# Retention states of the sample tokens: outer products on TensorE, or spread rows and DVE

## The reference

```
S_new[d, e] = gamma * S[d, e] + k[d] * v[e]
o[e]        = sum over d of q[d] * S_new[d, e]
```

## Time and profile before

| what | value |
|---|---|
| median of three runs | 935.5 us |
| the profiled execution | 933.9 us |
| its span in the trace | 932.3 us |
| PE busy in the span | 806.9 us (87%) |
| DVE busy | 429.8 us (46%) |
| ACT busy | 219.1 us (23%) |
| POOL busy | 73.9 us (8%) |

### The profile page before, as it was taken

One profiled execution on the slowest core, in us unless ns is written; L12 is line 12 of the kernel. 1 busy time (PEld: TensorE's weight loads), 2 busy tenths in 40 slices (PEclk: granted clock), 3 DMA queues, 4 the chain that ended last, 5 costly groups with the idle time before them and its releaser, 6 DMA issues. The chain is left out here.

```text
span 932.3 us, 13436 instructions
## 1 busy us (share of the span) xinstructions
PE 806.9 (87%) x5047; PEld 573.3 (61%) x5047; DVE 429.8 (46%) x994; ACT 219.1 (23%) x445; POOL 73.9 (8%) x71
## 2 busy tenths in 40 slices
PE   3689999999999999999999998937677788777984
PEld 2467887877977878878878876511653344324421
DVE  3153556547547546546555565782421232123224
ACT  3132505405314324324235041001100000000002
POOL 0000000000000000000000008950000000000000
PEclk9899999999999999999999999978589898889887
DMA  9834224224124224233242140110899999999961
GB/s 285 250 98 138 84 69 117 67 67 139 49 65 138 72 85 116 69 94 90 67 119 87 67 171 9 70 72 23 338 414 416 417 420 416 416 415 419 418 271 47
DMA packets 112603, 167.49 MB, mean 180 GB/s; under 512 B 7633, under 2 KB 91691, under 8 KB 103996
## 3 DMA queue, kind: packets, MB, share of 16 engines
q1 hardware_dynamic: 108876, 158.96, 47.3%
q0 software_dynamic: 1664, 4.98, 1.8%
q10 hardware_dynamic: 2032, 3.13, 1.0%
HBM read 158.63 MB, written 8.43 MB: 179 GB/s over the span
## 5 line engine op out<-in xcount | busy, mean ns | idle before, releaser
L275 PE MATMUL bank<-room,wall 128*128 128x264 f32 (+1 forms) x1152 | 287.2, 395 | 11.2 <-PEq L140 7.2
L275 PEld LDWEIGHTS bank<-room,wall 128*128 128x128 f32 x1152 | 212.3, 192 | 57.0 <-issue 15.3
L1553 PE MATMUL bank<-ring,xg 128*32 128x512 f32 x512 | 72.7, 732 | 35.5 <-DMA ring<-in_expert_w_up_dram 34.5
L1553 PEld LDWEIGHTS bank<-ring,xg 128*32 128x32 f32 x512 | 20.4, 132 | 87.0 <-issue 87.0
L1529 PEld LDWEIGHTS bank<-G,xn 128*128 128x128 f32 x384 | 44.9, 197 | 9.6 <-issue 5.9
L1529 PE MATMUL bank<-G,xn 128*128 128x128 f32 x384 | 46.4, 283 | 3.6 <-DVE GW L1777 3.6
L1805 DVE SCALAR_TENSOR_TENSOR th<-th,bank 128x256 f32<-128x256 f32 x8 | 3.4, 421 | 97.1 <-ACT th L1651 97.1
L1590 PE MATMUL bank<-y,GT 128*128 128x512 f32 x96 | 45.8, 612 | 1.0 <-issue 0.9
L275 PE MATMUL bank<-wall,merged 128*128 128x512 f32 (+1 forms) x96 | 44.4, 613 | 2.5 <-DVE merged L1314 2.5
L1794 DVE TENSOR_TENSOR x<-x,bank 128x512 f32<-128x512 f32 (+1 forms) x48 | 32.8, 684 | 12.2 <-PE bank L1590 12.2
L1112 POOL DMA_DIRECT2D out_rwkv_p_dram<-zout x8 | 4.9, 616 | 397.3 <-ACT zout L836 396.6
(11 more groups left out here) (366 smaller groups left out, 1316.4 us busy)
## 6 DMA issues: line engine op xcount, KB each, us to landing
wall<-in_w_in_dram SPq DMA_DIRECT2D x72, 512.0 KB, 3.6
ring<-in_expert_w_gate_dram SPq DMA_DIRECT2D x32, 1024.0 KB, 17.6
ring<-in_expert_w_up_dram SPq DMA_DIRECT2D x32, 1024.0 KB, 18.6
ring<-in_expert_w_down_dram SPq DMA_DIRECT2D x32, 1024.0 KB, 22.8
room<-in_state_ret_dram SPq DMA_DIRECT2D x8, 512.0 KB, 4.8
out_ret_s_dram<-room POOLq DMA_DIRECT2D x8, 512.0 KB, 3.8
wall<-in_w_out_dram SPq DMA_DIRECT2D x8, 512.0 KB, 3.5
room<-in_state_rwkv_dram SPq DMA_DIRECT2D x1, 2048.0 KB, 8.6
```

Of the source, the lines that this page charges most:

```text
L275: return nc.tensor.matmul(out, lhsT, rhs, start=start, stop=stop, skip_group_check=loose)
L1553: last = mm(MB[e * CAP:(e + 1) * CAP, :], xg[:, b, kk, e * CAP:(e + 1) * CAP], w, start=(kk == 0), stop=(kk == KT - 1))
```

## The change

The value rows alone are transposed (the key column is used where it stands, one channel per partition). ACT copies them to v8 and POOL writes v8 to a scratch row in memory, waits until it has landed, and loads it back spread over all 128 partitions as vrows (128 x 1024). ACT scales sin_ by gamma in place. DVE then forms snew with eight instructions of 128 columns, each with one column of kr as its scalar. On TensorE the outer products are gone and both halves of GB stand ahead of the snew wait; on ACT the tanh of GB stands ahead of the os_ copy; on DVE the snew step stands behind the sample copies (L1066) and the back part's merge (L1070 to L1077). In out_pass the two new DMAs stand between the zout store and the stp store. The constant diag8 and its load (L335) are gone.

The diff, without the lines on that constant:

```diff
@@ -452,8 +447,9 @@
         kvt = buf("kvt", [P, 4, P])
         vd = buf("vd", [P, TT, P])
         sc = buf("sc", [P, TP + P])
-        ks8 = buf("ks8", [B, 2, P])
-        vdiag = buf("vdiag", [B, B, P])
+        v8 = buf("v8", [B, P])
+        vrows = buf("vrows", [P, B, P])
+        scr_v = nc.dram_tensor("scr_v", [KT, B * P], F32, kind="Internal").ap()
         stp = buf("stp", [P, P])
         os_, osq, ors = ys, ysq, yrs
         oc = tok("oc")
@@ -729,8 +725,7 @@
                 for m, src in enumerate((kr[:, 0:P], kr[:, P:TP], vr[:, 0:P], vr[:, P:TP])):
                     last = nc.tensor.transpose(v4(M[3])[:, m, :], src, ident[:])
                 last.then_inc(sem("kvt_mm"), 1)
-                nc.tensor.transpose(M[0][0:B, 0:P], kr[:, TP:T], ident[:])
-                nc.tensor.transpose(M[0][0:B, P:2 * P], vr[:, TP:T], ident[:]).then_inc(sem("kv8_mm"), 1)
+                nc.tensor.transpose(M[0][0:B, 0:P], vr[:, TP:T], ident[:]).then_inc(sem("v8_mm"), 1)
                 project(pe, i, U_GA, 1)
             if back:
                 past(pe, "y_sq", n)
@@ -743,16 +738,12 @@
                 done(pe, "vd_ready", i)
                 mm(pe, M[4][:, 0:P], kvt[:, 0, :], vd[:, 0, :], True, False)
                 mm(pe, M[4][:, 0:P], kvt[:, 1, :], vd[:, 1, :], False, True).then_inc(sem("stp_mm"), 1)
-                done(pe, "vdiag_ready", i)
-                vflat = vdiag[:].rearrange("b c d -> b (c d)")
-                mm(pe, M[0][:, :], ks8[:, 0, :], vflat[:, 0:512], True, True)
-                mm(pe, M[3][:, :], ks8[:, 0, :], vflat[:, 512:1024], True, True).then_inc(sem("kv_mm"), 1)
                 project(pe, i, U_GB, 0)
+                project(pe, i, U_GB, 1)
                 done(pe, "snew_ready", i)
                 for b in range(B):
                     last = mm(pe, M[5][:, TP + b:TP + b + 1], snew[:, b, :], qr[:, TP + b:TP + b + 1], False, True, True)
                 last.then_inc(sem("o_mm"), 1)
-                project(pe, i, U_GB, 1)
                 done(pe, "o_copy", i)
                 mm(pe, M[0][:, 0:T], mean128[:], os_[:], True, True).then_inc(sem("omean_mm"), 1)
 
@@ -835,10 +826,13 @@
                 act.wait_ge(sem("zout_free"), n)
                 A.copy(zout[:], M[0][0:HD, 0:P].rearrange("p (h c) -> p h c", h=2)).then_inc(sem("zt_copy"), 1)
             if front:
+                done(act, "v8_mm", i)
+                last_pass(act, "v8_sent", 16 * i)
+                A.copy(v8[:], M[0][0:B, 0:P]).then_inc(sem("v8_ready"), 1)
                 done(act, "kvt_mm", i)
                 A.copy(kvt[:], v4(M[3])).then_inc(sem("kvt_copy"), 1)
-                done(act, "kv8_mm", i)
-                A.copy(ks8[:], M[0][0:B, 0:2 * P].rearrange("p (n c) -> p n c", n=2)).then_inc(sem("ks8_ready"), 1)
+                act.wait_ge(sem("sin_in"), 16 * (i + 1))
+                A.activation(sin_, sin_, ACT.Copy, scale=dcol[:, 2:3]).then_inc(sem("sin_decayed"), 1)
             if back:
                 past(act, "yc_ready", n)
                 A.activation(ysq[:, 0:TP], yc[:, 0:TP], ACT.Square).then_inc(sem("y_sq"), 1)
@@ -852,10 +846,10 @@
                 done(act, "stp_mm", i)
                 last_pass(act, "stp_sent", i * 16)
                 A.copy(stp[:], M[4][:, 0:P]).then_inc(sem("stp_ready"), 1)
+                projected(act, i, U_GB)
+                A.activation(gb[:], pj[1][:, 0:T], ACT.Tanh, scale=0.5).then_inc(sem("gb_tanh"), 1)
                 done(act, "o_mm", i)
                 A.copy(os_[:], M[5][:, 0:T]).then_inc(sem("o_copy"), 1)
-                projected(act, i, U_GB)
-                A.activation(gb[:], pj[1][:, 0:T], ACT.Tanh, scale=0.5).then_inc(sem("gb_tanh"), 1)
                 done(act, "oc_ready", i)
                 A.activation(osq[:], oc[:], ACT.Square).then_inc(sem("o_sq"), 1)
 
@@ -1045,8 +1039,6 @@
                 done(dve, "kvt_copy", i)
                 V.tensor_scalar(vd[:, 0, :], kvt[:, 2, :], dcol[:, 0:1], None, mult)
                 V.tensor_scalar(vd[:, 1, :], kvt[:, 3, :], dcol[:, 1:2], None, mult).then_inc(sem("vd_ready"), 1)
-                done(dve, "ks8_ready", i)
-                V.tensor_tensor(vdiag[:], ks8[:, 1:2, :].broadcast_to([B, B, P]), diag8[:], mult).then_inc(sem("vdiag_ready"), 1)
                 done(dve, "gs_tanh", i)
 
                 V.scalar_tensor_tensor(out=sg[:], in0=thg[:], scalar=1.0, in1=pj[U_GS % 2][:, 0:T], op0=add, op1=mult).then_inc(sem("gs_silu"), 1)
@@ -1054,14 +1046,6 @@
                 past(dve, "y_root", n)
                 V.reciprocal(yrs[:, 0:TP], yrs[:, 0:TP]).then_inc(sem("y_inv"), 1)
             if front:
-                dve.wait_ge(sem("sin_in"), 16 * (i + 1))
-                last_pass(dve, "snew_sent", 16 * i)
-                done(dve, "kv_mm", i)
-                for half, bank in enumerate((M[0], M[3])):
-                    bs = slice(4 * half, 4 * half + 4)
-                    last = V.scalar_tensor_tensor(out=snew[:, bs, :], in0=sin_[:, bs, :], scalar=dcol[:, 2:3], in1=v4(bank), op0=mult, op1=add)
-                last.then_inc(sem("snew_ready"), 1)
-
                 for m, src in enumerate((r, ep, kmod, vx, kk, ba)):
                     V.tensor_copy(svec[:, bass.ds(i, 1), m, :].rearrange("p o b -> p (o b)"), src[:, TP:T]).then_inc(sem("svec_part"), 1)
             if back:
@@ -1077,6 +1061,13 @@
                 V.tensor_tensor(tile, tile, yc[:, 0:TP], add).then_inc(sem("prompt_merged"), 1)
             if front:
 
+                done(dve, "sin_decayed", i)
+                last_pass(dve, "snew_sent", 16 * i)
+                done(dve, "k_rope", i)
+                dve.wait_ge(sem("vrows_in"), 16 * (i + 1))
+                for b in range(B):
+                    last = V.scalar_tensor_tensor(out=snew[:, b, :], in0=vrows[:, b, :], scalar=kr[:, TP + b:TP + b + 1], in1=sin_[:, b, :], op0=mult, op1=add)
+                last.then_inc(sem("snew_ready"), 1)
                 if back:
                     past(dve, f"state{NCH - 1}", n)
                 V.tensor_copy(epc[:], ep[:, C - 1:TP:C])
@@ -1113,6 +1104,14 @@
                 eng.wait_ge(sem("zout_sent"), 16 * n)
                 eng.sem_inc(sem("zout_free"), 1)
             if i is not None:
+                settle(eng)
+                done(eng, "v8_ready", i)
+                eng.dma_start(scr_v[bass.ds(i, 1), :].rearrange("o (b v) -> (o b) v", b=B), v8[:]).then_inc(sem("v8_sent"), 16)
+                last_pass(eng, "snew_ready", i)
+                eng.wait_ge(sem("v8_sent"), 16 * (i + 1))
+                eng.sem_inc(sem("v8_there"), 1)
+                settle(eng)
+                eng.dma_start(vrows[:].rearrange("p b v -> p (b v)"), scr_v[bass.ds(i, 1), :].broadcast_to([P, B * P])).then_inc(sem("vrows_in"), 16)
                 settle(eng)
                 done(eng, "stp_ready", i)
                 eng.dma_start(o["ret_p"][0, 0][bass.ds(i, 1)].rearrange("o k v -> (o k) v"), stp[:]).then_inc(sem("stp_sent"), 16)
```

More of the change, by code:

```diff
@@ L112, in constants @@
     out["slot"] = np.tile(np.arange(CAP)[None, :], (P, 1)).astype(np.float64)
[L113 to L116, removed]
     return {k: np.ascontiguousarray(v.astype(np.float32)) for k, v in out.items()}
@@ L251, in mixer_phase @@
         scanm = buf("scanm", [P, T])
-        diag8 = buf("diag8", [B, B, P])
         lwa = buf("lwa", [P, T])
@@ L335, in _ @@
                 for n, t in (("rope", rope), ("retdec", retdec), ("retcol", retcol[:]), ("mk", mk[:]), ("mlo", mlo[:]),
-                             ("scanm", scanm[:]), ("diag8", diag8[:])):
+                             ("scanm", scanm[:])):
                     act.dma_start(t, k[n]).then_inc(sem("const_in"), 16)
@@ L352, in _ @@
                 act.activation(lgb[:], lgb[:], ACT.Tanh, scale=0.5).then_inc(sem("lora_tanh"), 1)
-                act.wait_ge(sem("const_in"), 16 * 14)
+                act.wait_ge(sem("const_in"), 16 * 13)
             @block.vector
```

## The result

The changed kernel takes 982.66 us (median of four runs, 980.22 to 986.51) against 935.6 (median of four runs of the kernel before): a ratio of 1.0506, with a 95% interval of 1.0468 to 1.0543. The forecast was 958 us with a range of 944 to 975. The direction was right, but the loss is 47 us where 22 were forecast, and the time lies above the range. The profiled execution took 981.8 us, with a span of 980.2.

The account below looks back on a forecast made before the run. TensorE was taken to bound the kernel, busy 65.1 of a pass's 66 us. Eight passes at 1.8 us plus 1.0 us for the clock add 22.4 to 933.9, making 956.3; the median lies 1.6 higher: 958 us, range 944 to 975.

Parts of the forecast that it names:

- outer products and one transpose gone: On PE, four outer-product instructions (1.91 us) and the key-column transpose (0.11 us) go: 2.02 us saved per pass.
- variance later, behind the back part's square: On PE, the back part's variance starts at 212.5 instead of 211.87, because ACT's new work delays the square.
- PE stops for snew: PE, done with GB at 217.9, waits until snew is ready at 220.9: 3.0 us per pass.
- last thin matmul no longer overlapped: On PE, the one-column matmuls count their full 1.95 us before the os_ copy: 0.14 us per pass.
- uncovered copy to os_: ACT's os_ copy, formerly hidden by GB's second half, now delays PE's mean: 0.04 + 0.38 + 0.04 us.
- wait for ACT's square gone: PE's wait at the variance opening a pass falls away, as the gates are through early: 0.41 us saved.
- clock at half: TensorE's clock drops to 1.2 instead of 2.4 GHz behind the stop: 1.0 us lost per pass.
- I take 1.0 us per pass, with the bounds 0 and 1.68: TensorE clock loss behind the 3.0 us stop, priced between tail stops of 1.08 us (no loss) and 4.11 us (1.68).
- I take 2.2, nearer to zout: POOL's 4 KB v8 store lands in 2.2 us, priced between zout's 1.9 and stp's 3.2.
- the stop without the clock: Rival: PE stops as forecast but its clock stays at full speed; 14 us lost, 950 us; chance 0.20.
- The slow transfers: Rival: v8 takes 3.2 us, rows 4.6, DVE 8 x 0.28, clock full price; 43 us lost, 978 us; chance 0.15.
- PE never stopping: Rival: snew is ready when GB is through, at 217.9; 1.2 us saved per pass, 926 us; chance 0.07.

Follow-up runs that it names:

- the run with the order alone: Kernel before, outer products kept, with both halves of GB ahead of the snew wait and GB's tanh ahead of the os_ copy: 943.29 us, ratio 1.0083.
- the run with four products: Changed kernel plus four products with unused results ahead of PE's snew wait, filling half the stop: 982.71 us, ratio 1.0504.
- the run with the early rows: Changed kernel with value transpose, v8 and sin_ scaling moved earlier and POOL's row transfers ahead of zout; DVE unchanged: 967.44 us, ratio 1.0331.
- the last run: Changed kernel with early rows, DVE's snew ahead of the reciprocal, GB's second half behind thin matmuls and its tanh behind the os_ copy: 919.75 us, ratio 0.9826.

## Why the prediction was wrong

The direction, the mechanism and the order of the causes held; two terms of the sum were too small. In the pass shown, from the sample transposes to the next pass's first transpose, PE took 317.99 - 296.02 = 21.97 us, against 226.33 - 209.98 = 16.35 in the kernel before: 5.62 us more, where 2.8 were forecast. The terms beside those of the forecast:

| term, us per pass | forecast | measured |
|---|---|---|
| outer products and one transpose gone | -2.02 | -2.02 |
| variance later, behind the back part's square | 0.63 | 0.64 |
| PE stops for snew | 3.0 | 3.98 |
| last thin matmul no longer overlapped | 0.14 | 0.14 |
| uncovered copy to os_ | 0.46 | 0.47 |
| wait for ACT's square gone | -0.41 | -0.41 |
| clock at half | 1.0 | 3.0 |

The 0.63 of the forecast is its 212.5 - 211.87, and the 0.14 is the 1.95 us of the thin matmuls against the 1.81 from their start to the next row. The forecast column makes its 2.8 us. The measured column makes 5.8, somewhat more than the 5.62, as PE's rows overlap; eight times 5.62 is 45 of the 47 us. The clock term is the sum of 0.98 on the thin matmuls, 0.59 on the mean and 1.4 on the first half projection, each against the same instructions of the kernel before.

**The step that failed is "I take 1.0 us per pass, with the bounds 0 and 1.68".** It read the price of the clock off the length of PE's stop, between a stop of 1.08 us that cost nothing and one of 4.11. Two things were wrong in that. The thin matmuls and the second wait, which the sentence names, were given no price of their own. In the run with the order alone they brought the clock down with no stop, in four of six passes, and half a stop in front of them (the run with four products) cost as much as a whole one. And 1.68 was no upper bound: in the run with the early rows the stop was 3.15 us, close to the 3.0 of the forecast, and the clock took 3.9 us of the pass. Behind the 4.11 us stop of the tail came products of 128 columns, while in the changed kernel the thin matmuls and the copy came first, and the clock stayed down for 7 us, about 3 us lost. That the slow stretch is long because it begins with thin work fits these rows, but no run varied it by itself, so it is not shown.

The page "TensorE: Matmul & The Clock Gate" of the Trainium skill, in its section on why this matters for kernels, advises against idle gaps between bursts of matmuls if the throughput is to hold. The changed kernel agrees, with the clock at 0.50 behind a stop of 3.98 us. The run with the order alone goes further: PE's row showed it busy up to a wait of 0.47 us, and the clock fell.

**The stop was a third too short in the forecast.** Of the microsecond, 0.7 is the store of 4 KB: "I take 2.2, nearer to zout" was the wrong neighbour. It landed 2.9 us after issue in most passes, close to stp's 3.2. In the last run, where it is issued some 5 us before the zout store, it landed after 1.6 us (median). The weight loads beside it may make the difference, but no run changed them alone, so the cause of the longer landing stays open. Another 0.2 is DVE's step: 2.19 us for eight instructions, 0.27 each, near the upper bound of 0.28. The spread load, 4.0 us forecast, had a median of 4.0.

Of the rivals, the stop without the clock (950 us) fell with the granted clock of 0.93 to 0.95. The slow transfers (978 us) came near the time by luck: their stop was 4.8 us and their clock 1.68, where the pass shown has 3.98 and 3.0. PE never stopping was placed at 926 us, and the reason against it, that DVE is through with its merge too late however fast the rows are, is what the run with the early rows shows. Moving rows and DVE both brings that side, 920 to 923 us.

## What to carry to other kernels

Taking work off the engine that sets the pace pays only if what replaces it is ready by the time the engine asks for it: trace the new value back through every queue that it now passes, here POOL's list and DVE's place behind a reciprocal, and start it where its source is ready rather than where the old code stood. Keep full matmuls on both sides of thin ones and of short waits, and when pricing a stop on TensorE count the thin work next to it with the stop.

## What the hardware showed that was not expected

- Sixteen one-column matmuls with a wait of 0.47 us behind them brought the clock to 1.2 GHz in some passes (four of six), with no longer stop near them. With full products around them and no stop it stayed at 2.4 GHz in all; behind a stop of 2.05 us (the first pass of the last run) it fell although full products came behind the thin ones.
- A stop of 3.15 us cost more at the lower clock (3.9 us) than one of 3.98 us in another kernel (3.0 us).
- Filling a stop of 4 us with products that nobody reads made the kernel 17 us faster; filling half of it gained nothing.
- A store of 4 KB took 1.6 to 1.7 us to land in some places of a pass and 2.8 to 3.5 in others.
